# A PEER encoder layer: tables over 26 up blocks per tile, and rows of the down stage dealt one, two, then three per block

## The reference, cut to what matters

```python
def peer(xn, wq, subkeys, u, v):
    ...
    v1, i1 = lax.top_k(s1, PEER_TOPK)
    v2, i2 = lax.top_k(s2, PEER_TOPK)
    cand = (v1[..., :, None] + v2[..., None, :]).reshape(t, PEER_HEADS, PEER_TOPK * PEER_TOPK)
    sc, ci = lax.top_k(cand, PEER_TOPK)
    ...
    def block(args):
        xb, ib, gb = args
        a = jnp.einsum('td,tkd->tk', xb, u[ib]).astype(jnp.float32)
        act = (jax.nn.gelu(a, approximate=False) * gb).astype(xb.dtype)
        return jnp.einsum('tk,tkd->td', act, v[ib])
```

## Time and profile before

| | us |
|---|---|
| median of 3 runs | 2435.35 |
| lowest and highest | 2428.57, 2440.18 |
| the profiled execution's own time | 2437.25 |
| its span, first to last instruction | 2435.5 |
| up block 0 to the end of the up stage, from the first matmul of L980 | 840.8 to 1607.3 |
| down stage, PE | 1627.7 to 2293.0 |
| tail | 2293.0 to 2435.5 |

### The profile page before, as it was taken

The page is one execution under the profiler, slowest core; times in us unless marked ns, Lnnn a source line. Parts: engine busy times, 40 slices in busy tenths (PEclk is TensorE's granted clock), DMA queues, the critical chain, the costliest instruction groups (busy, mean ns, idle before and its releaser), DMA issues.

```text
span 2435.5 us, 27329 instructions
## 1 busy us (share of the span) xinstructions
PE 2268.7 (93%) x9992; PEld 1127.4 (46%) x9992; DVE 1796.6 (74%) x3557; ACT 788.1 (32%) x1222; POOL 776.7 (32%) x617
## 2 busy tenths in 40 slices
PE   7989998998879989999999999959999999999897
PEld 5445743445435434445545454424444444444443
DVE  3350087678656588999999997768888898888373
ACT  4241112115221124454444454423323332333203
POOL 0000100211437601232333254435444545444150
PEclk9988999999889999999999999979999999999998
DMA  5313412223569945878878799999999999999261
GB/s 173 137 69 120 166 69 87 97 77 121 166 241 346 329 153 186 334 253 309 309 284 296 266 356 357 368 396 386 389 388 387 388 389 385 385 380 346 98 232 53
DMA packets 244053, 625.41 MB, mean 257 GB/s; under 512 B 18640, under 2 KB 84560, under 8 KB 232656
## 3 DMA queue, kind: packets, MB, share of 16 engines
q1 hardware_dynamic: 146544, 275.49, 32.2%
q0 software_dynamic: 75776, 274.76, 31.0%
q10 hardware_dynamic: 21600, 73.41, 7.6%
HBM read 547.05 MB, written 76.55 MB: 256 GB/s over the span
## 4 chain that ended last, share of the span: by engine, by line
PE 59%; DVE 25%; DMA 7%; POOL 3%; ACT 3%; issue 2%; SPq 1%; DVEq 0%; ACTq 0%
PE ps L1025 27%; PE ps L739 18%; PE ps L980 5%; DVE arena L1689 4%; DVE arena L1586 4%; DMA arena<-peer_u,pk 3%; POOL arena L676 3%; PE ps L840 3%; DVE arena L1769 2%; DMA arena<-peer_v,pk 1%; DVE pk L1612 1%; DVE pk L1609 1%; DVE arena L1765 1%; DVE arena L1766 1%; SPq L583 1%
## 5 line engine op out<-in xcount | busy, mean ns | idle before, releaser
L980 PE MATMUL ps<-arena 128*128 128x512 bf16 x3072 | 684.7, 383 | 22.2 <-DVE arena L1586 18.7
L1025 PE MATMUL ps<-arena 128*128 128x512 bf16 x3072 | 665.3, 380 | 20.3 <-DVE arena L1795 20.3
L676 POOL DMA_INDIRECT arena<-peer_u,pk x256 | 367.2, 1434 | 642.7 <-DVE pk L1689 580.7
L739 PE MATMUL ps<-arena 128*128 128x512 f32 (+2 forms) x1552 | 554.7, 515 | 6.8 <-ACT arena L1074 2.8
L676 POOL DMA_INDIRECT arena<-peer_v,pk x256 | 362.6, 1416 | 434.6 <-DVE arena L1704 399.3
L1025 PEld LDWEIGHTS ps<-arena 128*128 128x128 bf16 x3072 | 300.4, 98 | 385.2 <-issue 23.6
L980 PEld LDWEIGHTS ps<-arena 128*128 128x128 bf16 x3072 | 298.5, 98 | 379.7 <-DVE arena L1586 24.0
L739 PEld LDWEIGHTS ps<-arena 128*128 128x128 f32 x1552 | 287.0, 194 | 255.6 <-issue 238.4
L1704 DVE SCALAR_TENSOR_TENSOR arena<-arena,pk 128x1024 f32<-128x1024 f32 x256 | 328.3, 1282 | 77.5 <-DMA arena<-peer_v,pk 69.9
L1689 DVE CUSTOM_DVE_ANT_0 arena<-arena 128x1024 f32<-128x1024 f32 x256 | 308.2, 1219 | 104.2 <-DMA arena<-peer_u,pk 103.2
L1345 ACT ACTIVATE arena<-arena 128x1024 bf16<-128x1024 f32 x128 | 134.7, 1054 | 447.7 <-PE ps L1025 269.0
(11 more groups left out here) (179 smaller groups left out, 1607.9 us busy)
## 6 DMA issues: line engine op xcount, KB each, us to landing
arena<-uT SPq DMA_DIRECT2D x128, 512.0 KB, 5.3
arena<-peer_v SPq DMA_DIRECT2D x64, 1024.0 KB, 15.6
scr_gelu<-arena ACTq DMA_DIRECT2D x128, 256.0 KB, 5.4
scr_gates<-arena ACTq DMA_DIRECT2D x16, 2048.0 KB, 10.8
arena<-scr_gelu SPq DMA_DIRECT2D x64, 512.0 KB, 11.8
arena<-scr_gates SPq DMA_DIRECT2D x32, 1024.0 KB, 16.3
arena<-w_in SPq DMA_DIRECT2D x14, 2048.0 KB, 8.0
arena<-peer_wq SPq DMA_DIRECT2D x8, 2048.0 KB, 11.3
```

The lines of the kernel that those rows point to most:

```text
L676: g.indirect_dma_start(out=u_rows[place], out_offset=None, in_=peer_u if r < NS * NSLOT else peer_v, in_offset=bass.IndirectOffsetOnAxis(a ...
L739: mm = nc.tensor.matmul(out, lhs(c), rhs(c), start=(c == 0), stop=(c == n - 1))
L980: mm = nc.tensor.matmul(ps[:, n % 2, :], w[n % 4][:, c, :], x[:, c, :], start=(c == 0 and w is uh and x is xh), stop=(c == DC - 1 and w is ...
L1025: mm = nc.tensor.matmul(ps[:, 2 * t + half, :], abf[b][:, pa, k, t * P:(t + 1) * P], vbf[b][:, pv, k, half * 512:half * 512 + 512], start= ...
```

## The change

Four numbers of the tables change. A tile has 26 up blocks instead of 27, so the fourth tile begins at block 92 instead of 95 and ends with block 117 instead of 121. In the first three tiles each block has one dot (before, every sixth had two), in the fourth two and three in turn (before two), and in the last ten up blocks one and two steps in turn (before three). With that the up stage has the same 150 dots and 4 rows instead of 10. `plan_down` deals the other 221 rows (before 215) by shares: 1 for each of the first eight down blocks, 2 for the next 104, 3 for the next 14, none in the last two. A share is worth 221 / 258 of a row: 6 rows in the first eight blocks, 1.71 per block in the middle, 36 rows in blocks 112 to 125. No instruction of another kind is added or removed, and the tail is the same.

```diff
-TILE_SLOTS = 27
+TILE_SLOTS = 26
...
             if t + 1 == ND:
-                at[n0 + i] += take(sparse, 2)
+                at[n0 + i] += take(sparse, 2 + i % 2)
             else:
-                at[n0 + i] += take(sparse, 1 + (i % 6 == 5))
+                at[n0 + i] += take(sparse, 1)
...
     for n in range(FIRST + ND * TILE_SLOTS, NK - 1):
-        at[n] += take(sparse, 3)
+        at[n] += take(sparse, 1 + n % 2)
     return at, sparse
+
+
+def plan_down(left):
+
+    share = [1] * 8 + [2] * (NK - 24) + [3] * 14 + [0] * 2
+    at, done = [], 0
+    for n in range(NK):
+        upto = len(left) * sum(share[:n + 1]) // sum(share)
+        at.append(left[done:upto])
+        done = upto
+    return at
...
-DOWN_PLAN = [LEFT[len(LEFT) * n // (NK - 2):len(LEFT) * (n + 1) // (NK - 2)] for n in range(NK - 2)] + [[], []]
+DOWN_PLAN = plan_down(LEFT)
```

## The result

The changed kernel takes 2441.62 us (median of 19 runs, 2438.11 to 2448.62), the kernel before 2432.8 us beside it (19 runs, 2428.26 to 2440.77). The ratio is 1.0042, with a 95% interval of 1.0033 to 1.0052: 8 to 13 us slower. The profiled execution took 2440.04 us, its span is 2438.3 us.

The account below looks back on a forecast made before the run. DVE's own time and the arrival of gathered rows were taken as limits beside PE. Profiled 2437.25 + 2.7 (later down start) + 6 (its end) = 2446.0 us, the median 1.9 lower: 2444, own range 2438 to 2450, overall 2420 to 2458.

Parts of the forecast that it names:

- Part 1: First three tiles of 26 blocks: DVE loses 6.9 us per tile, so it enters the fourth tile 20.7 us earlier.
- The entry that I named, near 1389: Sign in the profile after: the table step of the fourth tile is entered near 1389 us.
- Part 2: Fourth tile, 65 dots instead of 54 in 26 blocks: 185 us at 2.84 us per row, range 161 to 193.
- first rival: Fourth tile: bandwidth limits, not gathered rows' places; 161 to 165 us there, 2416 us in all, chance 0.14.
- within 6% of that limit: Fourth tile before the change: one row per 2.99 us used, against 2.84 us that four places allow.
- my formula: Time per gathered row: (1.15 us use + 1.7 notice and issue + landing) / places; 2.84 us in the fourth tile.
- halfway rival: Landings shorten to 8.0 us: fourth tile 177 us, down stage 5.3 us early, 2433 us in all, chance 0.26.
- Idle DMA: Claim from the tail, where nothing else moves: even with idle DMA a gather lands in 5.5 us.
- Part 3: From block 118 to the first down block: 56 us, set by loads; down stage begins 2.7 us later.
- Part 4: Down stage's last blocks, 36 rows instead of 24 in blocks 112 to 125: PE waits 6 us, 0 to 12.
- The one in which the end decides: Rival: landings pass 9 us; fourth tile 193 us, 12 us lost at the down stage's end, 2458, chance 0.18.

Follow-up runs that it names:

- e4: The kernel before with three places for gathered rows instead of four in its fourth tile; 2446.45 us in one run, the kernel before at 2429.64 beside it.
- e5: The changed kernel with six places for gathered rows instead of four in the fourth tile; 2422.83 us, ratio 0.9967 to the kernel before.
- e12: The kernel before, tables untouched, with six places for gathered rows instead of four in its fourth tile; 2421.45 us, ratio 0.9951.
- e2: The kernel before with only the changed kernel's table of down-stage rows; 2435.19 us, ratio 1.0009.
- e7: The changed kernel with six places in the fourth tile and the down-stage rows dealt evenly as before; 2415.86 us, ratio 0.9949.
- e10: e7 with ScalarE's cast of the first down block's product moved ahead of the fifth `peer_v` cast; 2416.78 us, ratio 0.9941.

## Why the prediction came out right, and where it was off

**The forecast** was 2444 us, its own range 2438 to 2450; measured 2441.62. Of the 2.4 us, 2.5 are the base: the three runs shown had a median of 2435.35, the 19 beside the changed kernel 2432.8. By difference, 8.7 us were forecast, 8.8 is the difference of the medians. The parts, from the profiles, each from block 14 on:

**Part 1, 20.7 us gained over three tiles.** Measured 22.3 (479.1 against 456.8). DVE enters tiles at 1230.51 and 1382.35, 151.8 us apart, where 151.6 was worked out. The tile is DVE's: 148.5 us of its work, no wait of it for anything, and no wait of PE for builds. The remaining 1.6 us may be the waits for the tables and for `coef`, which I counted at nothing; no run took them alone. The entry that I named, near 1389, was 1382.35, by the same 1.6 and by an execution that had reached block 14 5.4 us earlier. As a sign it was badly chosen: it should have been a distance, not a time of day.

**Part 2, 185 us for the fourth tile.** Measured 181.6. The mechanism held: DVE's work is 146.0 us (145.7 worked out), its waits for rows 35.6 (39 forecast), and e4, e5 and e12 show that the places set them. The sum beneath the 185 did not hold, and that it came out near is luck. I counted the issue's 1.4 us twice, since the 8.5 us of landing begin with the issue (see e4). Put right, (1.15 + 0.3 + 8.5) / 4 = 2.49 us per row would have made 162 us of the tile, the first rival's number, and "within 6% of that limit" would have read 17%. What I left out, the landed row's wait for its turn, the issue's wait for the one ahead and the gathers that land late, came to about as much as I had counted twice. With the landing as measured, 8.2 us, my formula gives 65 x (1.15 + 1.7 + 8.2) / 4 = 179.6. The 181.6 lie between the forecast and the halfway rival, nearer to the forecast. The 161 to 165 us of the rival that bandwidth decides came only with six places (e5). The Trainium skill's fit ("DMA: Bandwidth & Descriptors", section on the anatomy of one DMA on the gpsimd path), as an estimate 3.2 us for one gather of 512 KB, is not what the runs show: 6.6 us with three places, 8.2 with four, 9.9 with six. "Idle DMA" was not quite what the earlier trace rows show either: in the tail nothing but the gathers moves, yet two to four of them are on their way most of the time and bring 258 GB/s. The first of them, alone, landed in 5.3 us:

```profile
arena<-peer_v,pk POOLq DMA_INDIRECT x1, 5.3
```

PE's 30 us of waits in this tile were 17.8, in nine pieces of up to 4.2 us. The rest of its loss was its clock, which I hadn't counted at all; see the last section.

**Part 3, 56 us to the first down block.** Measured 61.5: the start of the chain of loads is the term that I set too early. SP's queue there, against the earlier trace rows, and ScalarE and PE, against the earlier trace rows:

```profile
1544.53 37.23 SPq L577 DMA_DIRECT2D arena<-uT  x7
1581.88 1.24 SPq L583 DMA_DIRECT2D arena<-peer_v  x2
1583.22 2.67 SPq L589 DMA_DIRECT2D arena<-scr_gelu  x4
1586.00 26.97 SPq L594 DMA_DIRECT2D arena<-scr_gates  x2
1613.02 4.33 SPq L583 DMA_DIRECT2D arena<-peer_v  x2
```

```profile
1611.68 0.60 ACT L1318 ACTIVATE arena<-ps 128x512 f32<-128x512 f32 x1 [4.58 <-PE ps L991]
...
1612.76 3.90 ACT L1356 ACTIVATE arena<-arena 128x1024 bf16<-128x1024 f32 x4 [0.48 <-ACT arena L1318]
1623.00 1.06 ACT L1356 ACTIVATE arena<-arena 128x1024 bf16<-128x1024 f32 x1 [6.34 <-DMA arena<-peer_v]
```

```profile
1575.15 36.43 PE L991 MATMUL ps<-arena 128*128 128x512 bf16 x165 [1.38 <-DVE arena L1597]
1625.44 4.42 PE L1036 MATMUL ps<-arena 128*128 128x512 bf16 x10 [13.86 <-DVE arena L1806]
```

PE's end was right: 1611.58, 47.6 us behind DVE's entry of block 118 (47.3 worked out). The loads were late. I let their chain begin 12 to 15 us behind block 118, since the last gate write leaves ten blocks before the end of the up stage. But SP takes its queue in order, and ahead of the readback stand the last loads of `uT`, each of which waits for the split of the block four before its own. They ended at 1581.9, so the readback began at 1586.0, 22 us behind block 118. From there it took 37.0 us to the fifth cast of `peer_v` (36 of bytes and 5 of latency worked out), with DMA at 389 GB/s, and 2.4 more to PE. The wait that I took away, that for the gate write, was replaced by the next one on the same queue. This is read from the one profile; no run moved the readback ahead of those loads, so what that would give is open. For the same reason PE's wait before the down stage was 13.9 us and not 8 to 12.

**Part 4, 6 us in the last down blocks.** Measured 6.5. DVE at the first block of the wait, and PE:

```profile
2235.28 1.28 DVE L1715 SCALAR_TENSOR_TENSOR arena<-arena,pk 128x1024 f32<-128x1024 f32 x1
2240.32 1.28 DVE L1715 SCALAR_TENSOR_TENSOR arena<-arena,pk 128x1024 f32<-128x1024 f32 x1 [3.76 <-DMA arena<-peer_v,pk]
2243.94 1.28 DVE L1715 SCALAR_TENSOR_TENSOR arena<-arena,pk 128x1024 f32<-128x1024 f32 x1 [2.33 <-DMA arena<-peer_v,pk]
```

```profile
2229.71 14.84 PE L1036 MATMUL ps<-arena 128*128 128x512 bf16 x67
2247.71 1.23 PE L1036 MATMUL ps<-arena 128*128 128x512 bf16 x4 [3.16 <-DVE arena L1806]
...
2270.95 26.26 PE L1036 MATMUL ps<-arena 128*128 128x512 bf16 x117 [0.68 <-DVE arena L1806]
```

Two of three rows in one block come late, and DVE's lead is gone; PE stands at 2244.6, which is block 119 of the stage, where I had said behind block 118. The place and the sum are as worked out, the kind isn't quite: only 3.8 us are waits, and most of the other 2.7 is the clock again. From the product's split of block 112 to that of block 119 DVE took 51.8 us (50.4 worked out), from there to that of block 126 39.0 (41.4). But the rate of a row per 2.8 us behind the 50.4 has the issue in it twice, as in part 2; with 2.5 DVE would have fallen 13.6 us behind, against a lead of 13, and I would have put PE's wait at under 1 us. That the size is right is luck for that reason, and also since e2 shows 3.1 for the same table.

**The rivals.** The one in which the end decides (2458) is out: landings in the down stage were 8.9 us, not above 9. The one of bandwidth is out for this kernel; for one with six places its number fits, and no run shows more.

## What to carry to other kernels

Work that waits for gathered rows has a rate of its own. Its ceiling is places / (use + notice + landing), worked out from three rows of a trace, with the landing counted from the start of the issue; with four and three places the real rate was 14 to 21% below that here, for a landed row waits for its turn and some land late. When DVE waits for rows and its rate is that near the ceiling, try more places before any other spread of the work, and take a formula that comes close for shown only when each of its terms is. Here two more places gave 0.5% with the tables unchanged (e12, 0.9951) and the change's tables added nothing to that which the intervals tell apart (e7, 0.9949; e10, 0.9941). Their profiles say otherwise, and this is open: from block 14 to the end of the down stage e7 takes 1346.3 us, e10 1346.9 and e12 1351.9. When a wait is removed from an in-order queue, look for the next wait of the same queue before counting the gain, and give signs as distances between two events of one profile.

## What the runs showed of the hardware

**Short waits of PE cost twice.** In before the granted clock was 1.00 over the fourth tile, and over the down stage too, but for its first 14 us, behind the wait of 20.35 us (columns: us, PE busy us, clock, DMA share, GB/s):

```profile
1627.69:1642.00 14.31, 14.31 (x57) 0.85 1.04 398
```

In the fourth tile and the down stage of after it fell behind each wait of 2.94 us and more, and behind none of 1.90 us and less. PE in order of time, in the fourth tile; the 16 matmuls of one unit take 1.1 us at the full clock. A clock of 1.00 is the upper of its two levels, 2.4 GHz; a figure below it is a mean over a stretch that holds both, 2.4 and 1.2 GHz.

```profile
1475.73 1.09 PE L1003 MATMUL ps<-arena 128*128 128x128 bf16 x16 [1.90 <-DVE arena L1780]
...
1487.48 1.89 PE L1003 MATMUL ps<-arena 128*128 128x128 bf16 x16 [3.79 <-DVE arena L1780]
...
1528.28 6.97 PE L991 MATMUL ps<-arena 128*128 128x512 bf16 x24 [4.22 <-DVE arena L1597]
...
1555.57 1.89 PE L1003 MATMUL ps<-arena 128*128 128x128 bf16 x16 [2.94 <-DVE arena L1780]
```

and stretches of PE alone (us, busy us, granted clock, DMA share, GB/s), one behind the second of these waits, one behind the wait of 3.16 us in the down stage:

```profile
1487.30:1494.30 7.00, 6.76 (x36) 0.76 0.83 285
```

```profile
2247.00:2258.00 11.00, 10.07 (x39) 0.84 0.86 264
```

Behind waits of up to 1.9 us the 16 matmuls still take 1.1 us, behind 2.94 and 3.79 us they take 1.9 (in e7 1.7 behind a wait of 2.08), and a block of 24 takes 7.0 us in place of 5.3 behind 4.22 us. At before's 159.98 / 930 = 0.172 us per weight load the 912 of the fourth tile would be 156.9 us of work; PE was busy 162.7 of 181.6. So 5.8 us of its loss there are clock, and 19.0 are time in which it stood. At the end of the down stage 3.8 us of waits came with 2.7 us that are left by difference; 0.84 over 11 us explains 1.8 of them, and a first 14 us at 0.82 instead of before's 0.85 some 0.5 more.

**A gather landed the later, the more places there were.** Median from the start of the issue to the landing in the fourth tile: 6.6 us with three places (321 GB/s in all), 7.5 to 8.5 with four (345 to 361), 9.4 to 9.9 with six (382 to 395). An added place is thus worth less than its share, but it still gave 19 us here, from four to six. Whether the number on their way or the traffic makes them late these rows don't tell, since both grow together, and it isn't all: in the third tile of before, with 290 GB/s and only 32 x 7.1 / 158.5 = 1.4 gathers on their way on average, they landed in 7.1 us, later than in e4 with 55 x 6.6 / 182.5 = 2.0 and 321 GB/s.
